# Two turns at a time on TensorE in the stick-breaking attention

## The reference, cut to what matters

```
z = einsum('bqhd,bkhd->bhqk', q, k) / sqrt(D_HEAD)
mask = k_pos[None, :] < q_pos[:, None]
log_1m = where(mask, -softplus(z), 0)
later = cumsum(log_1m, reverse) - log_1m
w = where(mask, exp(log_sigmoid(z) + later), 0)
out = einsum('bhqk,bkhd->bqhd', w, v)
```

## Time and profile before

| | us |
|---|---|
| three timed runs | 3123.06, 3123.10, 3121.51 (median 3123.06) |
| the profiled execution | 3127.81 |
| its span | 3126.1 |
| stretch of A | about 625 to 1085 from the start of the span |

### The profile page before, as it was taken

One profiled execution on the slowest core, in us unless ns is written; L12 is line 12 of the kernel. 1 busy time (PEld: TensorE's weight loads), 2 busy tenths in 40 slices (PEclk: granted clock), 3 DMA queues, 4 the chain that ended last, 5 costly groups with the idle time before them and its releaser, 6 DMA issues.

```text
span 3126.1 us, 45380 instructions
## 1 busy us (share of the span) xinstructions
PE 2948.2 (94%) x18136; PEld 2608.3 (83%) x18136; DVE 1639.5 (52%) x2275; ACT 960.5 (31%) x1621; POOL 328.9 (11%) x504
## 2 busy tenths in 40 slices
PE   6999789989999999868999999999999999999999
PEld 4678678888888899866899999978999998788887
DVE  4545244357666568863444544445444454455554
ACT  3322145545555422112322222223222222232221
POOL 1222110011000145650000000000000000000000
PEclk9999899999999999988999999999999999999999
DMA  6652322246222445324221121142112112443332
GB/s 209 192 195 95 109 79 72 70 138 183 70 78 79 138 144 159 93 65 147 89 81 54 62 74 55 61 155 94 55 54 81 54 57 93 140 146 122 132 125 86
DMA packets 284773, 327.28 MB, mean 105 GB/s; under 512 B 53357, under 2 KB 234191, under 8 KB 284563
## 3 DMA queue, kind: packets, MB, share of 16 engines
q1 hardware_dynamic: 284562, 324.37, 31.8%
HBM read 256.28 MB, written 67.78 MB: 104 GB/s over the span
## 4 chain that ended last, share of the span: by engine, by line
PE 52%; DVE 1%; DMA 1%; ACT 1%; issue 0%; SPq 0%; ACTq 0%; DVEq 0%
PE mf_psO L2112 26%; PE mf_psT L2164 22%; PE mf_psO L2164 1%; PE mf_psO L2135 1%; DMA mf_nat<-scratch_mix 1%; PE mf_psT L2098 1%; DVE mf_wlo L1980 1%; ACT mf_whi L1909 1%; PE mf_psO L2147 0%; DVE mf_acc L2063 0%; DVE mf_acc L2075 0%; ACT mf_hs L1962 0%; DVE mf_acc L2003 0%; DVE mf_hs L2009 0%; SPq L1843 0%
## 5 line engine op out<-in xcount | busy, mean ns | idle before, releaser
L2063 DVE TENSOR_TENSOR mf_acc<-mf_psO,mf_acc 128x1024 f32<-128x1024 f32 x256 | 313.5, 1225 | 368.3 <-PE mf_psO L2112 368.0
L2164 PE MATMUL mf_psT<-mf_xhi,mf_wlo 128*128 128x384 f32 (+1 forms) x1440 | 459.7, 319 | 0.0
L2164 PE MATMUL mf_psT<-mf_xlo,mf_whi 128*128 128x384 f32 (+1 forms) x1440 | 459.6, 319 | 0.0
L2164 PE MATMUL mf_psT<-mf_xhi,mf_whi 128*128 128x384 f32 (+1 forms) x1440 | 459.4, 319 | 0.0
L2112 PE MATMUL mf_psO<-mf_whi,mf_uhi 128*128 128x512 f32 x1024 | 405.5, 396 | 10.5 <-DVE mf_acc L2063 6.6
L2112 PE MATMUL mf_psO<-mf_wlo,mf_uhi 128*128 128x512 f32 x1024 | 402.9, 393 | 0.0
L2112 PE MATMUL mf_psO<-mf_whi,mf_ulo 128*128 128x512 f32 x1024 | 402.4, 393 | 0.0
L1909 ACT ACTIVATE mf_whi<-mf_st 128x2048 fp32r<-128x2048 f32 x108 | 206.2, 1912 | 535.5 <-PE mf_psO L2112 509.4
L2164 PEld LDWEIGHTS mf_psT<-mf_xhi,mf_whi 128*128 128x128 f32 x1440 | 270.5, 188 | 1.6
L2164 PEld LDWEIGHTS mf_psT<-mf_xlo,mf_whi 128*128 128x128 f32 x1440 | 270.5, 188 | 1.6
L2164 PEld LDWEIGHTS mf_psT<-mf_xhi,mf_wlo 128*128 128x128 f32 x1440 | 270.5, 188 | 0.0
(11 more groups left out here) (207 smaller groups left out, 5501.9 us busy)
## 6 DMA issues: line engine op xcount, KB each, us to landing
mf_st<-in_w_up SPq DMA_DIRECT2D x48, 1024.0 KB, 5.3
mf_st<-in_w_down SPq DMA_DIRECT2D x48, 1024.0 KB, 6.6
md_wst<-in_w_in SPq DMA_DIRECT2D x24, 1024.0 KB, 5.3
pj_wst<-in_w_in SPq DMA_DIRECT2D x18, 1024.0 KB, 6.8
scratch_proj<-pj_ob SPq DMA_DIRECT2D x48, 256.0 KB, 2.0
mf_st<-in_w_o SPq DMA_DIRECT2D x12, 1024.0 KB, 6.1
pj_xin<-in_x_prompt SPq DMA_DIRECT2D x16, 512.0 KB, 5.5
md_qn<-scratch_proj SPq DMA_DIRECT2D x64, 128.0 KB, 2.7
```

The source lines that it names most:

```text
L2063: nc.vector.tensor_tensor(acc[0:r, i, :], psO[k % 2][0:r, :], acc[0:r, i, :], ALU.add).then_inc(s["o_out"], 1)
L2164: last = nc.tensor.matmul(up_psum(t, f, b, cn), wa[b4][:, w0:w0 + P], xa[:, j, c0:c0 + cn], start=j == 0 and q == 0, stop=j == KD - 1 and ...
```

## The change

PE's generator of `attention` is cut into local functions for scores, bias, keys and queries, values, back, and weight transposes. For B they are called as before. For A an even turn issues nothing, and the odd turn behind it does both turns, kind by kind: scores of both, then keys and queries of both, values of both, back of both, weight transposes of both. The quantum of D that stands behind the even turn keeps its place in the list. The other engines' streams, the buffers and the semaphores are the same.

```diff
--- before.py
+++ after.py
@@ -1109,8 +1109,7 @@
     def tensor(pe):
         if before:
             before.done(pe)
-        for turn in TURNS:
-            i = turn
+        def scores(i):
             if 0 <= i < NU:
                 s, h, k0, w, _, _ = units[i]
                 seq, t0, r, _ = steps[s]
@@ -1131,6 +1130,8 @@
                         last = nc.tensor.matmul(psZ[i % ZB][0:r, x0:x1], qq[q][:, h, 0:r],
                                                 KT[:, h, c0 + x0:c0 + x1], start=first, stop=not first)
                 last.then_inc(z_ready, 1)
+
+        def turn_bias(turn):
             h = turn - BIAS
             if not A and 0 <= h < H:
                 if h == 0:
@@ -1142,6 +1143,8 @@
                     x1 = min(BW, x0 + 512)
                     last = nc.tensor.matmul(psZ[0][:, x0:x1], flip[:, :], btr[:, h, x0:x1], start=True, stop=True)
                 last.then_inc(turned, 1)
+
+        def keys_and_queries(turn):
             i = prep_step.get(turn)
             if i is not None:
                 seq, t0, r, att = steps[i]
@@ -1162,7 +1165,8 @@
                 for h in range(H):
                     last = nc.tensor.transpose(psT[:, h, 0:r], qn[i % 2][0:r, h, :, :], ident[0:r, 0:r])
                 last.then_inc(qT_ready, 1)
-            j = turn - L_AV
+
+        def values(j):
             if 0 <= j < NU and j % 2:
                 s, _, k0, w, first, last_ = units[j]
                 seq, t0, r, _ = steps[s]
@@ -1184,6 +1188,8 @@
                                                 wT[jj % 4][0:kr, b, 0:r],
                                                 start=first and b == 0, stop=last_ and b == nb - 1)
                 last.then_inc(av_done, 1)
+
+        def back(turn):
             for s in due(turn, L_BACK):
                 r = steps[s][2]
                 pe.wait_ge(oT_ready, att_no[s] + 1)
@@ -1195,7 +1201,8 @@
                 for pair in range(H // 2):
                     last = nc.tensor.transpose(psT[0:r, pair, :], oT[:, pair, 0:r], ident[:, :])
                 last.then_inc(back_ready, 1)
-            j = turn - L_T
+
+        def turn_weights(j):
             if 0 <= j < NU:
                 s, h, k0, w, _, _ = units[j]
                 r = steps[s][2]
@@ -1207,6 +1214,33 @@
                     last = nc.tensor.transpose(psW[j % WB][0:kr, b, 0:r],
                                                flipped[j % NW][0:r, b * P:b * P + kr], ident[0:r, 0:r])
                 last.then_inc(wT_ready, 1)
+
+        if not A:
+            for turn in TURNS:
+                scores(turn)
+                turn_bias(turn)
+                keys_and_queries(turn)
+                values(turn - L_AV)
+                back(turn)
+                turn_weights(turn - L_T)
+                yield
+            return
+
+        for turn in TURNS:
+            if turn % 2 == 0 and turn + 1 in TURNS:
+                yield
+                continue
+            both = [z for z in (turn - 1, turn) if z in TURNS and (z == turn or turn % 2)]
+            for z in both:
+                scores(z)
+            for z in both:
+                keys_and_queries(z)
+            for z in both:
+                values(z - L_AV)
+            for z in both:
+                back(z)
+            for z in both:
+                turn_weights(z - L_T)
             yield
 
     stage = Stage(len(TURNS), sync, gpsimd, scalar, vector, tensor)
```

## The result

The changed kernel takes 3141.26 us (median of 4 runs, 3135.72 to 3143.57), the kernel before 3123.08 in the same comparison; the ratio is 1.0054, 95% interval [1.0038, 1.007]. The forecast was 3143.5. The profiled execution took 3142.85; its span is 3141.1, 15.0 more than before.

The account below looks back on a forecast made before the run. PE's in-order stream was taken to bound attention A, any new wait paid in full. Terms -2.5 + 16.0 + 8.0 - 1.1 = +20.4 us on the 3123.06 median gave 3143.5 us, range 3118 to 3163.

Parts of the forecast that it names:

- Part 2: Attention A, last 16 tiles: query transposes wait on PE for ACT's copy of the keys, 1.00 us each, +16.0 us.
- The rival that it has no effect: ACT's key copy is there in time, so PE's query transposes do not wait; about 3122 us, chance 0.12.
- Part 3: Attention A: ACT's copies and sigmoids come bunched, so a body's second scores wait for the sigmoid; +8 us.
- The heavy queue: Rival: ACT's bunched work costs 0.30 us in every pair of attention A, 25 us; 3160 us, chance 0.16.
- Parts 1 and 4: PE in attention A: one full-precision visit per pair instead of two, -2.5 us; key transposes' wait for `o` goes, -1.1 us.
- one visit less: PE in attention A: dropping the odd turn's own full-precision visit saves 0.03 us per pair over 84 pairs, -2.5 us.
- The rival of the issue gaps: PE's issue gaps before values and weight transposes are the price of alternating, grouping halves them; 3114 us, chance 0.12.

Follow-up runs that it names:

- e1: Changed kernel with a body's query transposes issued behind its values instead of right behind the key transposes; 3126.1 us, ratio 1.0009.
- e3: Kernel before, nothing grouped, with the query transposes of the 16 later tiles following the key transposes in the same turn; 3138.91 us, ratio 1.0054.
- e7: Changed kernel with ACT copying the transposed keys of the 16 later tiles once more, ahead of the copy the queries wait for; 3148.82 us, ratio 1.0089.
- e5: Changed kernel with ACT's sigmoid of a turn placed before the copy of the transposed weights in attention A; 3132.66 us, ratio 1.0033.
- e2: Changed kernel with query transposes behind the values and ACT's sigmoid ahead of the copy of transposed weights; 3121.2 us, ratio 0.9998.
- e4: As e2, but a body's first weight transposes stand between its two groups of scores, giving two full-precision visits per pair; 3124.01 us, ratio 1.0003.
- e6: Kernel before, nothing grouped, with the values of two pairs of turns issued together every fourth turn in attention A; 3115.69 us, ratio 0.9979.

## Why the prediction was right, step by step

It was right in direction, in the main cause and in size: +18.2 us by the medians against +20.4. The closeness of the size is in part luck. In the stage the terms came to 12.8, 6.4 and -2.7 where 16, 8 and -3.6 were forecast: each was too large, and the saving offset a part of it. And the profiles, from which the terms were added up, show +16.5 in the stage and +15.0 in the span, less than the medians do. Two of the terms are near for other reasons than the forecast gave.

- *Part 2, the key wait:* forecast 16.0. In the trace 16 x 0.87 = 13.9; e1 takes 12.8 out of the stage, e3 puts 14.6 in. The number of waits was exact. The size was off mostly at the handover: I had taken DVE's 0.15 from the earlier trace rows, from ACT's copy it is 0.05; the way to the copy took 0.64, not 0.67. The rival that it has no effect is out by e1, e3 and e7. What was said for that rival, that ACT idles over half of this stage, was misread: the earlier trace rows has ACT busy for 161.65 of 300 us.
- *Part 3, ACT's bunch:* forecast 8. e5 takes out 6.9 in the stage and 6.2 in its inner part, e2 against e1 6.4 and 6.2. As an estimate of an excess over a slack it was the weakest term, and came out near by luck: it put 3.2 of its 8 us on the 16 bodies with a query copy, and expected most of the waits there. Only 4 of the 16 waits have one, with 2.0 of the 7.8 us of PEld's waits; the others stand behind dense work on ACT. Why most bodies with a query copy stay without a wait is open. The heavy queue (25 us) is out.
- *Parts 1 and 4, grouping and the wait for `o`:* forecast -3.6 together, e2 gives -2.7 in the stage. The wait for `o`, -1.1, went as forecast. The -2.5 for one visit less did not come: in the inner part at most 0.6 of it is seen (e2), and the second visit costs 0.4 there (e4). It stood on a difference of 0.03 between starts that are printed to 0.01, times 84. What came in its place is the 1.8 us at the beginning of the stage, with fewer us at the lower clock, which no part of the forecast had. The rival of the issue gaps is out: "issue" ahead of the values still totals 23.1 us over 73 times in the changed kernel (21.4 over 68 in the earlier trace rows), and ahead of the weight transposes 10.4 over 59 (11.7 over 67).
- *Sum, in the inner part:* 11.4 (e1) + 6.2 (e2 against e1) - 1.1 (e2 against before) = 16.5; the steps of a chain of kernels must add up so. The spans of the two profiles differ by 15.0: the stage by 16.5, what lies ahead of it by 1.1, what lies behind it by -2.6. The medians differ by 18.2, from four runs each, with an interval of about 12 to 22 us. The list of waits in the earlier trace rows begins at 660 us; between 625 and 660 PE also waits 3.9 us for `khl` (L1021), and 4.8 in two waits in the changed kernel.
- *That the dear seams are those at the ends of the 128x64 products* and not the changes of precision: e6 left the number of precision changes and halved the groups of values, and the time fell. The 0.17 also stands between products of the same precision: ahead of values that follow query transposes (894.60 above), and behind values that are followed by the turning back of a finished step:

```profile
PEld md_psT L1202 <- issue: 2.7, 16, 0.2
```

This is the tiling-mode rule of the Trainium skill ("TensorEngine Tiling (Array Packing)", Key Properties), that a change of the mode drains the array; the runs agree with it, at 0.11 and 0.17 us per group. That it is the tile's width and nothing else of these products that costs was not isolated.

## What to carry to other kernels

Before instructions of one kind are put together on an engine that works in order, look at what ran between a producer's copy and its next use: a gap that other work filled becomes a wait when the work moves, here 0.87 us for each tile, 16 times. The same holds for an engine that serves the group: it gets its work in a bunch, and the second half comes late although the engine is busy only half of the time (147.03 of 300 us). And measure a seam by starts in the timeline before regrouping for it: here the one that the change removed was worth 0.01 us at most, and the two at the ends of the values, which it left alone, 0.3 together. A difference of 0.03 us between two starts is too small to be multiplied by 84. To price a seam, compare kernels over a stretch in which the granted clock is the same: 1.6 of the 2.7 us that e2 gained lay outside such a stretch.

## What the runs showed that I had not expected

The handover from ACT to a waiting PE took 0.05 us (copy ended at 893.97, weights loaded from 894.01, first transpose at 894.02), a third of what the one DVE row had suggested. Holding back the first half of the values by two turns with only four weight buffers cost no wait on PE, although ACT waited for values 38 times there, 118.0 us in all between 700 and 1070 us:

```profile
ACT md_wT L952 <- PE md_psO L1183: 118.0, 38, 5.3
```
